# Two-block model step on one Trainium2 core: nine of the first block's gate products stand elsewhere in its recurrence stage, and the second block's mixing shares one program block with its neighbours

## What is computed

```python
# first block, hybrid_mixer
proj = h @ w_in
gates = sigmoid(proj[..., GATE_OFF:] + gate_b)                  # 4 x 1024 columns
y_c = rwkv7_mixer(proj[..., RW_OFF:SG_OFF], ...)                # 256-step recurrence
merged = gates[0] * (y_a @ sc_out) + gates[1] * (y_b @ sb_out) \
       + gates[2] * (y_c @ rw_out) + gates[3] * (y_d @ sg_out)

# second block
y = gelu(ssm_output)
y = y * sigmoid(y @ w_glu + b_glu)                              # end of the S5 branch
y_s, y_m = y @ w_ssm_out, mlstm_output @ w_ml_out
mixed = sigmoid(g_s) * y_s + sigmoid(g_m) * y_m
h = h + mixed @ w_out
h = h + peer_ffn(rmsnorm(h, norm2_g), peer_w_q, peer_sub_keys, peer_u, peer_v)
```

## Time and profile before

| what | value |
|---|---|
| median of 3 runs | 1773.02 us (1771.93 to 1781.65) |
| the profiled execution: its own time / its span | 1776.36 us / 1774.6 us |
| PE busy (matmuls) | 1671.4 us, 94% of the span |
| DVE, ACT, POOL busy | 64%, 45%, 19% |
| TensorE clock granted, mean over the span | 0.974 of full speed |
| moved by DMA | 289.44 MB, 163 GB/s over the span |

### The profile page before, as it was taken

One profiled execution on the slowest core, in us unless ns is written; L12 is line 12 of the kernel. 1 busy time (PEld: TensorE's weight loads), 2 busy tenths in 40 slices (PEclk: granted clock), 3 DMA queues, 4 the chain that ended last, 5 costly groups with the idle time before them and its releaser, 6 DMA issues. The chain is left out here.

```text
span 1774.6 us, 32796 instructions
## 1 busy us (share of the span) xinstructions
PE 1671.4 (94%) x11200; PEld 1516.3 (85%) x11200; DVE 1139.0 (64%) x2258; ACT 800.8 (45%) x1330; POOL 345.4 (19%) x220
## 2 busy tenths in 40 slices
PE   4989899979999999998899999999999999999997
PEld 4967897869999886777899999999999888888886
DVE  4453422657777594661439996677776577777776
ACT  3442111425554454223235655455555555555554
POOL 0030000004444000234736899000000000000000
PEclk9989999989999999999999999999999999999999
DMA  6502123425555422114434877555555766666673
GB/s 230 183 24 95 59 84 119 143 86 179 187 185 194 150 102 72 36 48 166 143 132 131 256 221 209 178 177 176 177 175 187 235 236 237 236 236 237 236 237 128
DMA packets 92804, 289.44 MB, mean 163 GB/s; under 512 B 10304, under 2 KB 27072, under 8 KB 92352
## 3 DMA queue, kind: packets, MB, share of 16 engines
q1 hardware_dynamic: 92304, 287.61, 49.7%
q10 hardware_dynamic: 432, 0.90, 0.1%
HBM read 270.64 MB, written 17.83 MB: 163 GB/s over the span
## 5 line engine op out<-in xcount | busy, mean ns | idle before, releaser
L259 PE MATMUL psum<-arena_parts 128*128 128x256 f32 (+2 forms) x1664 | 479.9, 288 | 33.7 <-DVE ring_parts L254 12.3
L261 PE MATMUL psum<-arena_parts,ring_parts 128*128 128x256 f32 (+1 forms) x1600 | 452.5, 283 | 0.0
L2558 DVE TENSOR_TENSOR ring_parts<-ring,arena_parts 128x512 fp32r<-128x512 f32 x418 | 282.8, 690 | 116.0 <-ACT arena_parts L2358 96.1
L259 PEld LDWEIGHTS psum<-arena_parts 128*128 128x128 f32 x1664 | 317.9, 191 | 37.1 <-issue 23.9
L261 PEld LDWEIGHTS psum<-arena_parts,ring_parts 128*128 128x128 f32 x1600 | 306.0, 191 | 0.0
L260 PE MATMUL psum<-h_parts,arena_parts 128*128 128x256 f32 x1024 | 287.6, 281 | 0.0
L254 POOL TENSOR_TENSOR ring_parts<-ring,arena_parts 128x1024 fp32r<-128x1024 f32 x79 | 208.7, 2661 | 88.4 <-ACT arena_parts L250 71.0
L230 PE MATMUL psum<-h,ring 128*128 128x256 f32 x896 | 209.6, 393 | 0.0
L2327 PE MATMUL psum<-arena_parts,x_parts 128*128 128x512 f32 x512 | 202.0, 395 | 2.7 <-DVE x_parts L2585 2.7
L2328 PE MATMUL psum<-ring_parts,x_parts 128*128 128x512 f32 x512 | 201.1, 393 | 0.0
L2329 PE MATMUL psum<-arena_parts,x_parts 128*128 128x512 f32 x512 | 200.4, 391 | 0.0
(11 more groups left out here) (527 smaller groups left out, 2937.5 us busy)
## 6 DMA issues: line engine op xcount, KB each, us to landing
ring<-stream SPq DMA_DIRECT2D x473, 512.0 KB, 3.5
kept<-arena SPq DMA_DIRECT2D x128, 128.0 KB, 2.2
arena<-kept SPq DMA_DIRECT2D x32, 512.0 KB, 4.3
arena<-first SPq DMA_DIRECT2D x1, 2144.0 KB, 7.6
arena<-second SPq DMA_DIRECT2D x1, 1632.0 KB, 6.4
x<-x_t SPq DMA_DIRECT2D x1, 1024.0 KB, 5.8
out<-arena SPq DMA_DIRECT2D x4, 256.0 KB, 2.1
arena<-last ACTq DMA_DIRECT2D x1, 512.0 KB, 3.5
```

What stands on the lines that cost most here:

```text
L259: nc.tensor.matmul(dst, stationary[0], moving[0], start=first, stop=False)
L261: return nc.tensor.matmul(dst, stationary[1], moving[0], start=False, stop=last_one)
L2558: v.tensor_tensor(low[:, s, w], ring[:, s, w], expert_high[:, m % 2, w].bitcast(F32), ALU.subtract)\
```

## The change

Two things, with no instruction of computation added except a one-element square root on ACT.

1. *First block.* The 32 gate products are placed anew. Calls of `gate_products` before: 2, 0, 3, 3, 3, 0, ten single ones in the levels, 2, 3, 6. After: 3, 2, 3, 3, 3, 1, ten, 2, 3, 2. ACT's reads follow. ACT takes its square-root table by a dummy activation before it waits for `kk_sum`.
2. *Second block.* The three program blocks are one (most lines of the raw difference are this indentation). ACT's GELU stands between the third and the fourth of the six last `z_reads` and tells a semaphore `y_open`, which PE waits for. The first combination takes its slots as 6, 3, 5, with its `y5` product last, so only that one waits for `s5_gated`; its banks are 3, 4, 2. The first three output blocks run their k-steps 0 to 5 when three of four parts of `mixed` are there, and their k-steps 6 and 7 after the fourth. The first PEER query waits for `qx_low` one k-step at a time, and the norm's sum waits for ACT's squares.

```diff
 # ScalarE, first block
                 sca.tell(a.activation(sb_l, sb_l, ACT.Ln, bias=ones[:, 0:1]), S("sb_logs"))
+                gate_reads(act, 1)
                 act.wait_ge(S("rw_mixed"), 1)
...
                 sca.tell(a.activation(g_rw, b3(2), ACT.Copy), S("rw_sigmoids"))
+                gate_reads(act, 1)
+                a.activation(spare[:], ones[:, 0:1], ACT.Sqrt)
                 act.wait_ge(S("kk_sum"), 1)
...
-                gate_reads(act, 6)
+                gate_reads(act, 2)
 # TensorE, first block
                 ins.then_inc(S("sb_scores"), 1)
-                gate_products(pe, 2)
+                gate_products(pe, 3)
                 pe.wait_ge(S("lora_in"), 1)
...
                 ins.then_inc(S("rw_lora"), 1)
+                gate_products(pe, 2)
 
                 pe.wait_ge(S("kk_squares"), 1)
...
+                gate_products(pe, 1)
                 for lev in range(1, LEVELS + 1):
...
-                gate_products(pe, 6)
+                gate_products(pe, 2)
 # ScalarE, end of the S5 and mLSTM part
-                z_reads(act, 6, ACT.Sigmoid)
+                z_reads(act, 3, ACT.Sigmoid)
                 act.wait_ge(y_taken, ONCE + 4)
-                sca.link(a.activation(us[:, :, M:TT], us[:, :, M:TT], ACT.Gelu_apprx_tanh))
+                sca.tell(a.activation(us[:, :, M:TT], us[:, :, M:TT], ACT.Gelu_apprx_tanh), y_open, ONCE + 1)
+                z_reads(act, 3, ACT.Sigmoid)
 # mixing
-        combos = ((5, 6, 3), (0, 1, 2), (7, 4, 5), (6, 3, 0))
+            loaded = ((5, 6, 3), (0, 1, 2), (7, 4, 5), (6, 3, 0))
+            combos = ((6, 3, 5),) + loaded[1:]
+            GATE_AT, COMBO_BANKS, OPEN = (2, 0, 0, 0), ((3, 4, 2), (5, 6, 7), (2, 3, 4), (5, 6, 7)), 3
...
-        with nc.Block() as block:
...
+                pe.wait_ge(y_open, ONCE + 1)
                 project(pe, (7, 4), (0, 1), 1, gate)
-                pe.wait_ge(S("s5_gated"), 1)
                 pe.wait_ge(S("h_parts"), split["h"] + 1)
...
+                def onto(q, ks):
+                    s, b = cycle[q], q % 4
+                    if ks[0] == 0:
+                        pe.wait_ge(full[s], (pe_at.rounds[s] + 1) * 16)
+                        pe.wait_ge(drained[b], pe_at.banks[b] + q // 4 + 1)
+                    ins = parted(8 + q, bank[b], mixed_high, mixed_low, ks)
+                    if ks[-1] == KT - 1:
+                        ins.then_inc(used[s], 1)
+
+                pe.wait_ge(S("mixed"), 3)
+                for q in range(OPEN):
+                    onto(q, range(6))
                 pe.wait_ge(S("mixed"), 4)
-                project(pe, cycle, range(4), 1, onto)
+                for q in range(OPEN):
+                    onto(q, range(6, KT))
+                for q in range(OPEN, KT):
+                    onto(q, range(KT))
 # PEER, first query product
-        with nc.Block() as block:
...
+                            if m == 0:
+                                pe.wait_ge(S("h_parts"), split["h"] - KT + k + 1)
```

More of the change, by code:

```diff
@@ L2006, in _ @@
                         .then_inc(S("h_rounded"), 1)
-                    nc.scalar.activation(qx_squares[:, k, :], x[:, k, :], ACT.Square)
+                    ins = nc.scalar.activation(qx_squares[:, k, :], x[:, k, :], ACT.Square)
+                ins.then_inc(S("norm_squares"), 1)
             @block.gpsimd
@@ L2142, in build @@
-        n_norm = normed["n"]
-        normed["n"] += 1
-        scale_turned, h_scaled = S("sg_normed"), S("sb_suffix")
-        with nc.Block() as block:
+            split["blocks"] += 16
+            split["h"] += 1 + KT
+            normed["squares"] += 1
+            ge = Area(arena)
+            G = ge.take(P, T)
+            early = ge.take(EARLY, T)
+            parts = Area(arena_parts[ge.at])
+            h_high = parts.take(KT, T)
+            h_low = h_parts[:, :, 0:T]
+            expert_high = parts.take(2, D)
@@ new lines, in build @@
+            KEEP = 4
+            chosen = early[:, KEEP:KEEP + 3, :]
+            ap_ = Area(arena)
+            qp = ap_.take(16, T)
+            sc = ap_.take(2, 16, P)
+            work = ap_.take(4, T)
+            sv = ap_.take(2, 16, 16)
+            token_scale = ap_.take(2)
+            CANDIDATES = ((0, 0, 2, 16), (32, 2, 2, 8), (48, 4, 4, 4), (64, 8, 8, 2))
+            N_CAND = 80
+            lines = [(float(nb), float(start // nb - a0)) for start, a0, na, nb in CANDIDATES]
+            cand = ap_.take(8, N_CAND)
@@ new lines, in build @@
+            si_u = ap_.take(2, 16, 16).bitcast(U32)
+            ci_u = ci.bitcast(U32)
+            assert ap_.at <= 17152
+            ER = (3, 0, 1, 2, 7, 4, 5, 6)
+            WHOLE, QUADS = 47, T // 4
+            PLAIN = P - WHOLE - 1 - QUADS
+            U_BANKS, ROW_BANKS = (4, 5), (6, 7)
+            assert (WHOLE + 1) % 8 == 0 and PLAIN % 8 == 0
+            kept = nc.dram_tensor("kept", (P // 4, P, 4, T), F32, kind="Internal").ap()
+            ONCE = 1
+            stored = [S(name) for name in ("tm_done", "tm_read", "mv_done", "mv_read")]
@@ new lines, in build @@
+            acts_in = [S(name) for name in ("gh_done", "gh_read")]
+            act_gated, gate_rounded = S("gn_mean"), S("gn_var")
+            q_base = split["blocks"]
+            e_base = {s: pe_at.rounds[s] + QS.count(s) + (s in (1, 2)) for s in ER}
+            hots = [x[:, 4 * n:4 * n + 4, :].rearrange("p a t -> p (a t)").rearrange("p (c q n) -> p c q n", c=2, q=4)
+                    for n in range(2)]
+            gate_high, gate_low = x_parts[:, 0:4, :], x_parts[:, 4:8, :]
+            HALF = D // 2
@@ new lines, in build, with eights, ring_slot, uses @@
+            halves = (slice(0, HALF), slice(HALF, D))
+            def eights(eng, count, one):
+                if count >= 8:
+                    with eng.Fori(0, count // 8) as i:
+                        for q in range(8):
+                            one(q, i)
+                for q in range(count % 8):
+                    one(q, count // 8)
+            def ring_slot(q):
+                return ER[q % 8]
+            def uses(q, i):
+                return i + (e_base[ring_slot(q)] + q // 8 + 1)
```

155 lines of the change are left out of this document (55 added, 100 removed).

## The result

The changed kernel takes **1743.2 us** (median of 4 runs, 1739.3 to 1746.1), the kernel before 1775.2 (4 runs, 1771.9 to 1781.7) on the same chip: a ratio of 0.982, interval 0.980 to 0.984. That is 32 us faster, where 37.8 was forecast; the time lies inside the range and 8.0 us above the predicted 1735.2. A second comparison, on other executions, gave 0.981 (0.979 to 0.983). The profiled execution took 1744.8 us (span 1743.0), against 1776.4 (span 1774.6) before: 31.6 us less.

A forecast was written before the change was run, and what follows sets the result against it. PE, busy 94% of the span, was taken as the bound, with time won only at its pauses or low clock. First block 16.0 plus second block 21.8 gave 37.8 off 1773.0, so 1735.2 us; range 1728 to 1748.

The forecast's parts named there:

- The first block: Gate products moved from the block's end into PE's pauses: the next program block begins at about 300.8 us, 16.0 earlier.
- about 1.95: Ahead of the levels: L834 takes 1.95 us instead of 3.78, if a pause of about 1.8 leaves the clock up.
- The chain behind `kk_sum`: First block: `kk_root` comes at 134.7 us instead of 134.3, so the whole chain behind it moves 0.4 later.
- Entry and first combination: Start of the mixing: early GELU and products back to back bring PE to the next combination 9.7 us earlier.
- Output blocks: Early k-steps cover PE's 5.2 us pause for the fourth part of `mixed`; with 2.2 of low clock, 7.4 us.
- First query: Seven k-steps run over the 3.3 us pause for the last `x_low` and a barrier; with the clock, 4.7 us.
- exposed rest 0.3: First query: what remains of its pause after seven k-steps run over it, between 0 and 0.8 us, taken as 0.3.
- late weights: Rival, mixing: loads land late at the second low part and bunched refills, +5 to +8 us, so 1742; chance 0.08.
- pauses under another name: Rival, joined blocks: PE still waits for `mixed` 4 or at k-step 7, 5.2 + 3.3 us with their clock, 1745; chance 0.07.
- what is gained before 928 us should arrive at the end whole: From 928 us to the end: clock 1.00, PE busy 824.7 of 846.0 us, no pause the change could touch.
- the prediction's own signs: Among them: span 37 to 38 us shorter; prediction wrong if the clock falls behind the pauses that are left.
- The rival that the clock reacts to density: Rival: PE working without a break from 827 us brings 0.50 stretches behind 928 us; 120 us give 1796; chance 0.03.

The follow-up runs named there:

- before again: The kernel before, unchanged, measured and traced once more: 1777.1 us.
- both halves: Against the kernel before, only the first block's edits: 1757.8 us, ratio 0.9895; only the second block's edits: 1756.1 us, ratio 0.9893.
- the version with the product put back: Changed kernel with the gate product ahead of the levels moved back to the first block's end: 1746.7 us, 0.9833 of the kernel before.
- the pause at 8.71: Changed kernel with SyncE's request for the first kept activations three blocks later: 1749.9 us, 0.9848 of the kernel before.

## Why the prediction was right, and where it was off

*The first block*: forecast 16.0, found 14.9 in this pair of traces and 14.6 to 18.5 over all. The pauses ahead of `rw_lora` and `kk_sum` are gone, the group ran at 1.00, L839 took 2.05 for "about 1.95" behind a pause of 1.65 for "about 1.8", and DVE's last product ended at 299.76 for 299.8. The chain behind `kk_sum` moved 0.1 later (DVE's L576 at 134.47 for 134.36) and not 0.4. The 1.1 us that are missing stand at the end. The six products before took 21.79 us, 0.9 more than at full clock; the sum took four at full clock away from them (4 x 3.45 = 13.8) and so left two that end at 299.5. They took 9.11, to 300.67, since twice as much of the low clock fell on them. The prediction had no term for the clock in this place.

*Entry and first combination*: forecast 9.7, found 9.3 (26.4 - 17.1). *Output blocks*: forecast 7.4, found 7.5 (33.9 - 26.4). *First query*: forecast 4.7, found 3.9. The term "exposed rest 0.3" was 0.97, above its bound of 0.8 and above the 0.5 us that no pause up to there should pass: I had priced the last `x_low` without POOL beside it (the last two ended at 879.43, POOL's L254 at 878.76), though the Trainium skill's page on SBUF named above would have told to look for it. The bank that the first matmul waits for, which I had not named, is a second wait of the same length. The rivals on late weights and on pauses under another name fell: from 809.8 to 876 us PE has no pause.

*Between the two blocks* the lead rose from 14.9 to 17.1, though no instruction of PE differs there. The terms come to 35.6, and with these 2.2 the lead at the values is 37.8. These 2.2 are luck: the stage varies by 5.6 us over the fourteen traces.

*The step that failed*: "what is gained before 928 us should arrive at the end whole". I had read 1.00 from 928 us on and a full PE, and taken that for a property of the stage. But the stage has a 2.74 us pause for DVE at its middle, behind which the clock may or may not fall; the trace of before was one where it did not. Two of the prediction's own signs failed here: the span is 31.6 us shorter and not 37 to 38, and the clock fell behind a pause that was left. Of fourteen traces ten have this pause, and in six of them the clock was below 0.8 in the 7 us behind it (before again, the changed kernel twice, both halves, the version with the product put back); in four it was 1.00. With the pause at 8.71 it fell; in three with at most 0.79 it did not. By the rate of the ten, three traces without it would come by chance in one case of sixteen (0.4 x 0.4 x 0.4), so that the pause brings the low clock here is likely and not shown. The cost, 1.5 to 2.8 us by the length of the whole stage, belonged into the range as a draw for either kernel.

*The period of 2.800* is open. Three of the fourteen traces have it: the changed kernel twice and the version with the product put back. All three have the low clock at the start of the values; none of the seven without it does; but four traces with the low clock kept 2.773. All three have the edits of both blocks, which before and the halves (four traces) don't have. What decides it is not shown. No run tried to set the period by itself.

*Against the median* 2.2 us of the 8.0 are the kernel before itself, whose median was 1775.2 in this comparison and 1773.0 in the runs of which the prediction knew; the other 5.8 are about the loss in the values, 6.1 in the trace. The rival that the clock reacts to density falls: in the changed kernel's trace the clock is 1.00 from 806 us to 1370, with PE busy for 431.7 of the last 442.0 of these. (In six of the fourteen traces it fell once more, to a mean of 0.83 over 10 us, behind the pause of 2.2 us near 1085 us that all have: a second such draw, worth 1.5 us.) The rule named with it ("TensorE: Matmul & The Clock Gate" of the Trainium skill, section "What's actually happening": activity releases the clock) agrees with these rows.

The version with the lowest median, the changed kernel with ScalarE's order changed, takes 1735.8 us, 38 below before (ratio 0.979). Against the changed kernel it is 4 to 6 us by the ratios. Only 2.0 us of this are shown to be its doing: the pause (2.74 to 0.79). Its trace is 11.0 us shorter than the changed kernel's; of these 6.1 lie behind the first value matmul (the low clock and the period, which other versions with the full pause escape as well) and 3.0 ahead of the mixing, where nothing differs.

## What to carry to other kernels

A pause of some microseconds on the matmul engine is paid twice, once as idle time and once, in some executions and not in others, as slow matmuls behind it; so list every pause on the way to the end, those that the change does not touch too, before saying that a gain arrives whole. Put independent work into the pauses by order of their length, and look at each engine that feeds the pause for an instruction that sits idle in front of work that is ready: here the order of two steps on ScalarE took 2 us of pause away behind a change that gave 32. Undo a term to see it in the trace: the times alone could not tell 5 us apart here. And before you call a lead between two traces measured, find out how far the same landmark moves between two executions of one kernel: here by 1.4 to 2.5 us after 300 us.

## What the runs showed of the hardware

- *Ahead of the levels the clock followed the pause.* Behind 5.29 us the same group of matmuls took 3.78 or 3.79 us in all four traces that have this pause; behind 1.63 to 1.65 us it took 2.05 in all ten. That is no rule for every place: at the end of the first block the clock was 0.50 from 285.4 to 295.4 us, with no pause above 1.6 us in or ahead of that stretch since 191.5.
- *Ahead of the values it differs from execution to execution.* The same kernel, with the same 2.74 us pause, went on at 1.00 in one trace and at 0.55 in another; in ten traces with this pause it fell six times.
- *A small DVE operation is five times as long beside POOL.* L2069, 128x256 with fp32r output, took 0.47 us alone and 2.33 us where POOL had begun a TENSOR_TENSOR of 128x1024 just before, whose end it waited for by the rows.
- *Two periods of the same loop.* At full clock, without a wait, three 512-column matmuls take 0.693 us in eleven traces and 0.700 us in three, over the whole phase in each.
- *A table load is followed at once by its activation*: 1.29 to 1.30 us from start to start for a load of 1.28, in the rows above and in the earlier trace rows.
